# One core, two transformer-like blocks: ScalarE's order in the V projection, two DVE steps in stick-breaking attention, and one DMA for a broadcast

## The chip, the cores and the metric

The kernel runs on one core of a Trainium2 chip. The metric is the device time of one execution in microseconds (us); of several runs the median is given. The engines are TensorE (PE), VectorE (DVE), ScalarE (ACT), GpSimd (POOL) and SyncE (SP), which issues the weight loads. Each runs its own list of instructions in order and waits on semaphores for the others.

## The reference, cut to what matters

Two blocks follow each other, on 512 tokens of width 1024. The first has a mixer (a state-space part and a stick-breaking attention side by side), a cross attention to 256 memory tokens, and an MLP. The second, with 16 more tokens, has gated linear attention, sparse attention with a bias by distance, and two gated MLPs. What the change touches lies in the first block's mixer:

```python
def hybrid_mixer(hn, w_in, ...):
    proj = hn @ w_in
    z, xbc, dt_raw, qkv = jnp.split(proj, ...)
    xbc = silu(causal_dwconv(xbc, conv_w, conv_b))
    xs, bm, cm = jnp.split(xbc, ...)
    y = ssd_chunked(xh, dt, a, bm, cm)                 # 4 chunks of 128 tokens
    y = (y + d_skip * xh) * silu(z)
    y_ssd = rmsnorm(y, ssd_norm_g)
    q, k, v = jnp.split(qkv, 3, axis=-1)
    o = stick_breaking_attention(q, k, v)              # 8 heads of 64
    y_sb = rmsnorm(o, sb_norm_g)
    return concatenate([y_ssd, y_sb]) @ w_out

# stick-breaking, for s < t, with z = q k^T / 8:
# A[t,s] = sigmoid(z_ts) * prod_{s<j<t} (1 - sigmoid(z_tj));  out = A v

def memory_cross_attention(hn, mem, g_mem, w_q, w_k, w_v, w_o):
    m = rmsnorm(mem, g_mem)
    k, v = m @ w_k, m @ w_v
    ...

# second block, sparse attention: a bias by distance, one value per head and (key - query)
bias = rel_bias[rel_bucket(top_idx - qpos)]
```

## The kernel before, in words

All matrix products are float32 made of rounded parts: a value is split into a high part, `w_hi` or `x_hi`, and a low part, `w_lo` or `x_lo`, and PE adds hi x hi, hi x lo and lo x hi. Weights come in units of 128 x 2048 values. SP loads a unit into one of two places in `w_raw`, ACT makes `w_hi` (line 363), DVE `w_lo` (line 370), and PE multiplies (line 448). A layer has some units, a unit some tiles; tile (j, m) is tile m of unit j. A tile is summed in one of two PSUM slots, `lin[0]` or `lin[1]`, by turns, so PE starts a tile only when the tile before the last has been taken out (semaphores `lin_taken0` and `lin_taken1`).

The first block projects xbc, dt, z, q, k and v in that order, in float32 on 512 tokens. V is laid out with tokens in partitions: 2 units of 4 tiles, each 128 x 256, 24 matmuls a tile. ACT takes a tile into `v_tok` (line 905). Between the tiles other work is woven in, written by hand as tables `after={(unit, tile): step}`: for PE a step follows the tile, for ACT it goes ahead of the taking of the tile. In V these are, on ACT, the exponentials of the state-space part's last chunk (`act_ssd(act, 3)`: `seg`, `to_end`, `e_cum`), the Silu of z (`z_silu`, with its table load), the square roots of the memory norm (`act_memory_root`, with a table load), two constants copied to `sb_fixed`, the high parts of attention heads 0 and 1 (`act_sb_hi`: `sb_q`, `sb_k`), and the first logarithm (`act_sb_log`: `stay_e`). On PE they are the state-space step of chunk 3 with the sums of the memory norm after tile (0,2), and the logits of head 0 (`pe_sb_first`) after tile (1,0). DVE has a plain list in `dve_projections`: products of `q_t` and `k_t` with the norm's scale, low parts (`dve_sb_lo`), the state-space output (`dve_ssd_out`), the reciprocal of the memory norm (`dve_root`) and the products of `y_t` with the Silu.

The attention itself is `pe_stick`, `act_stick`, `dve_stick` and `pool_stick`, eight heads one behind the other. For each head PE makes logits (lines 1227 to 1231), ACT absolute value, exponential and logarithm (`stay_e`), DVE `stay`, ACT and DVE its two parts (`stay_hi`, `stay_lo`), PE the exponents (line 1247), ACT the weights `w_att`, and PE the product with `v_tok` (line 1257). PE fills its waits with other products in one PSUM bank, the fill bank: in heads 0 to 3 the memory's keys and values, in heads 4 to 7 the eight tiles of the state-space half of the output projection (`mixed`, line 1302). DVE empties the bank into `tmp` (line 1444), and PE may begin the next fill only then. After each pair of heads the output goes to `o_t`, ACT makes its `x_hi` (line 597) and DVE its `x_lo` (line 614).

POOL, in `pool_stick`, writes a vector of 655 distances for each of 8 heads, which lies in `tmp`, to DRAM, in 128 copies each (`rel_dram`): one small DMA from `tmp` to row 0 and, when that has landed, one DMA from row 0 to rows 1 to 127. DVE waits for them (`rel_kept`) before it overwrites `tmp` in head 4.

Of the kernel before, what the change touches and what calls it, by code (L numbers as in the profile page):

```python
# [23 lines left out]
P = 128  # L24
# [105 lines left out]
def build(nc, weights, x_t, mem_t, meta_t, cols, consts, w_a2b, rel_t, rel_dram, out):  # L130
# [4 lines left out]
    with ctx:  # L135
# [726 lines left out]
        def act_projections(act):  # L862
            def all_squares():
                for t in range(KD):
                    act_squares(act, l_mix, t, t % 2)

            act_evacuate(act, XBC, lambda j, i, m, s: nc.scalar.activation(
                conv_in[:, 4 * i + 2 * j + m, 3:3 + S1], psum_tile(s, S1), ACT.Copy),
                after={(0, 0): all_squares, (1, 1): lambda: act_root(act, l_mix)})
            next_hi(act, DT, 0, 0)  # L870

            def softplus():

                slot, before, _ = DT.tile(0, 0, 0)
                act.wait_ge(sem(f"lin_taken{slot}"), before + 1)
                bias = param("dt_bias", 0, 8)
                link(act, nc.scalar.activation(dt_row[:, 0, :], dt_row[:, 1, :], ACT.Abs, bias=bias))
                nc.scalar.activation(dt_row[:, 2, :], dt_row[:, 1, :], ACT.Relu, bias=bias)
                nc.scalar.preload_act_table_set("natural_log_exp_and_others")
                nc.scalar.activation(decay_rate[:, :], param("a_log", 0, 8), ACT.Exp)  # L880
                link(act, nc.scalar.activation(dt_row[:, 0, :], dt_row[:, 0, :], ACT.Exp, scale=-1.0))
                nc.scalar.activation(dt_row[:, 1, :], dt_row[:, 0, :], ACT.Ln, bias=1.0)\
                    .then_inc(sem("dt_log"), 1)

            def conv_silus():
                for t in range(6):
                    act.wait_ge(sem("conv_sum"), t + 1)
                    nc.scalar.activation(conv_out[:, t, :], conv_out[:, t, :], ACT.Silu)\
                        .then_inc(sem("conv_done"), 1)

            def z_silu():
                act.wait_ge(sem("z_scaled"), 1)
                nc.scalar.activation(zs[:, :, :], zs[:, :, :], ACT.Silu).then_inc(sem("z_silu"), 1)

            act_evacuate(act, Z, lambda j, i, m, s: nc.scalar.activation(
                zs[:, 2 * j + m, :], psum_tile(s, S1), ACT.Copy),
                after={(0, 0): softplus, (1, 0): conv_silus, (1, 1): lambda: act_ssd(act, 0)})
            act_evacuate(act, Q, lambda j, i, m, s: nc.scalar.activation(
                q_t[:, 4 * i + 2 * j + m, :], psum_tile(s, S1), ACT.Copy, scale=SB_SCALE),
                after={(1, 0): lambda: act_ssd(act, 1)})  # L900
            act_evacuate(act, K, lambda j, i, m, s: nc.scalar.activation(
                k_t[:, 4 * i + 2 * j + m, :], psum_tile(s, S1), ACT.Copy),
                after={(0, 1): lambda: act_ssd(act, 2), (1, 0): lambda: act_memory_squares(act, 0),
                       (1, 1): lambda: act_memory_squares(act, 4)})
            act_evacuate(act, V, lambda j, i, m, s: nc.scalar.activation(
                v_tok[:, m, (2 * i + j) * 256:(2 * i + j) * 256 + 256], lin[s][:, 0, 0:256], ACT.Copy,
                scale=scale_tok[:, 0, m:m + 1]),
                after={(0, 0): lambda: act_ssd(act, 3), (0, 2): z_silu, (0, 3): lambda: act_sb_first(act),
                       (1, 0): lambda: act_memory_root(act), (1, 1): lambda: act_sb_second(act),
                       (1, 2): lambda: act_sb_log(act, 0)})  # L910

        def dve_projections(dve):
            def scaled(t):

                return nc.vector.tensor_tensor(t, t, scale_d[:, 0:S1], ALU.mult)
# [63 lines left out]
            wait_taken(dve, K)  # L979
            for t in range(4):  # L980
                scaled(q_t[:, t, :])
                scaled(k_t[:, t, :]).then_inc(sem("qk_scaled"), 1)
            dve_sb_lo(dve, 0)
            dve_ssd_out(dve, 3)
            next_lo(dve, V, 1, 0)
            dve_root(dve, l_mem)
            dve_sb_lo(dve, 1)
            dve.wait_ge(sem("z_silu"), 1)
            for t in range(4):
                nc.vector.tensor_tensor(y_t[:, t, :], y_t[:, t, :], zs[:, t, :], ALU.mult)\  # L990
# [2 lines left out]
        def pe_projections(pe):  # L993
# [9 lines left out]
                                                (1, 0): lambda: pe_ssd_back(pe, 2),  # L1003
                                                (1, 1): lambda: pe_ssd_front(pe, 3)})
            pe_linear(pe, V, x_hi, x_lo, after={(0, 2): lambda: pe_memory_sums(pe),
                                                (1, 0): lambda: pe_sb_first(pe)})


        memory_sums, memory_tok = lin[0][:, 1, 0:256], lin[0][:, 1, 256:258]
# [15 lines left out]

        def act_memory_root(act):
            act.wait_ge(sem("square_sums"), l_mem.idx + 1)
            act.wait_ge(sem("qk_scaled"), 4)
            nc.scalar.activation(scale_d[:, 0:MEM], memory_sums, ACT.Sqrt, bias=eps_col(EPS1), scale=1.0 / D)
            nc.scalar.activation(scale_tok[:, 1, 0:2], memory_tok, ACT.Sqrt, bias=eps_col(EPS1), scale=1.0 / D)\  # L1030
                .then_inc(sem("square_root"), 1)
# [138 lines left out]

        def act_sb_hi(act, hd):
            (own, other, s), t = sb_halves(hd), hd // 2
            act.wait_ge(sem("qk_scaled"), t + 1)
            if hd >= 2:
                act.wait_ge(sem("sb_logits"), hd - 1)
            nc.scalar.activation(sb_q[s][own, :], q_t[own, t, :], ACT.Copy)
            nc.scalar.activation(sb_k[s][own, 0, :], k_t[own, t, :], ACT.Copy).then_inc(sem("sb_hi"), 1)

        def act_sb_first(act):

            for x, name in enumerate(("ident", "drop_upto")):
                nc.scalar.activation(sb_fixed[:, x, :], const(name), ACT.Copy)
            act_sb_hi(act, 0)

        def act_sb_second(act):

            nc.scalar.preload_act_table_set("natural_log_exp_and_others")
            act_sb_hi(act, 1)

        def dve_sb_lo(dve, hd):  # L1190
            (own, other, s), t = sb_halves(hd), hd // 2
# [214 lines left out]
        def dve_stick(dve):  # L1406
# [44 lines left out]
            for hd in range(8):  # L1451
# [9 lines left out]
                    split_lo(dve, XK.unit0 + (hd if hd < 5 else 5) + 1, 0, nc.vector)  # L1461
                if hd >= 2 and hd % 2 == 0:
                    output(hd // 2 - 1)
                if hd < 2:
                    memory_keys(hd)
                if hd >= 4:
                    mixed(2 * hd - 7)
                if hd < 7:
                    stay_low(hd + 1)
                if hd in (4, 5, 6):  # L1470
                    dve_operand(dve, l_sb, hd - 4)
                if hd < 2:
                    for t in (2 * hd, 2 * hd + 1):
                        dve_operand(dve, l_ssd, t)
# [869 lines left out]
        def pool_stick(pool):  # L2344
# [4 lines left out]
            def add_square(N, t):  # L2349
# [2 lines left out]
                acc = squares[:, N.slots[0], 0:N.n]  # L2352
                nc.gpsimd.tensor_tensor(acc, acc, tmp[:, t % 2, 0:N.n], ALU.add).then_inc(sem("square_added"), 1)

            pool.wait_ge(sem("qk_scaled"), 4)
            pool.dma_start(rel_dram[:, 0:1, :], rel_vec.unsqueeze(1)).then_inc(sem("rel_row"), 16)
            pool.wait_ge(sem("square_added"), l_mem.added0 + l_mem.k)
            pool_sb_other(pool, 0)
            pool.wait_ge(sem("rel_row"), 16)
            pool.dma_start(rel_dram[:, 1:P, :], rel_dram[:, 0:1, :].broadcast_to([8, P - 1, VEC]))\  # L2360
                .then_inc(sem("rel_kept"), 16)
            pool_sb_other(pool, 1)
            clear(l_ssd, l_mix.idx + 1)
            pool.wait_ge(sem("square_added"), l_ssd.added0)
# [353 lines left out]
```

## Time and profile before

| | us |
|---|---|
| median of 3 runs | 2100.66 |
| lowest, highest | 2099.49, 2101.15 |
| the profiled execution | 2099.49 |
| its span (first to last instruction) | 2097.7 |
| PE busy in it | 2013.8 |
| DVE busy | 1051.5 |
| ACT busy | 745.5 |
| POOL busy | 248.5 |

The times in the rows are those of the profiled execution, from the start of its span. The mean granted clock of PE was 0.978 of full speed, 2.4 GHz. A matmul's busy time overlaps that of its neighbours; the step from one start to the next tells what it costs. "Idle before" in square brackets is the time that the engine stood still ahead of an instruction, with the instruction that ended it.

### The profile page before, as it was taken

Reading aid. Unit: us, or ns where it says so; the run is one execution under the profiler, and the core shown is the slowest. Engines: PE = TensorE matmul, PEld = TensorE weight load, DVE = VectorE, ACT = ScalarE, POOL = GpSimd, SP = SyncE. Lnnn points to the kernel's source line nnn. Section 1 sums busy time; section 2 is a strip of 40 time slices with the busy share of each in tenths; the row PEclk is TensorE's granted clock in tenths of the full one; section 3 lists DMA queues with packets and bytes.
Section 4 is the critical chain, followed back from the end, with each engine's and each line's share of the span. In section 5 each row is a group of like instructions: output and inputs, shape, how many; then the busy total and the mean of one; then the engine's idle time right before and its main releaser. Section 6 shows DMA issues by size and latency. Waiting matters only on the chain.

```text
span 2097.7 us, 28613 instructions
## 1 busy us (share of the span) xinstructions
PE 2013.8 (96%) x11546; PEld 1725.7 (82%) x11546; DVE 1051.5 (50%) x1348; ACT 745.5 (36%) x941; POOL 248.5 (12%) x208
## 2 busy tenths in 40 slices
PE   8999988999999999999999999999997899999996
PEld 6788765788888878998999999998884588888885
DVE  6668665544444544131543434345897553444434
ACT  4449734423132443223332222223535442222122
POOL 2012230200000210013100000001245010000001
PEclk9999999999999998998999999999998999999998
DMA  4223211222222221111222222222121022222221
GB/s 173 101 81 114 71 49 41 100 90 92 101 99 82 101 81 52 69 41 41 81 81 100 81 100 81 98 83 101 61 91 51 21 86 95 101 96 84 101 100 60
DMA packets 27823, 174.67 MB, mean 83 GB/s; under 512 B 4409, under 2 KB 4537, under 8 KB 7762
## 3 DMA queue, kind: packets, MB, share of 16 engines
q1 hardware_dynamic: 25680, 167.32, 22.5%
q0 software_dynamic: 1888, 5.90, 0.9%
q8 instruction: 71, 1.16, 0.2%
q14 instruction: 22, 0.18, 0.0%
q10 hardware_dynamic: 162, 0.10, 0.0%
HBM read 171.19 MB, written 4.78 MB: 84 GB/s over the span
## 4 chain that ended last, share of the span: by engine, by line
PE 70%; issue 20%; DVE 5%; ACT 3%; POOL 2%; DMA 1%; SPq 0%; POOLq 0%; DVEq 0%; ACTq 0%
PE lin L448 57%; PE aux L1302 1%; PE aux L2176 1%; POOL squares L629 1%; ACT w_hi L363 1%; PE aux L1745 1%; PE aux L1759 1%; PE lin L1257 1%; PE lin L2146 1%; PE aux L2160 1%; DMA w_raw<-in_weights 1%; PE aux L1286 1%; DVE w_lo L370 1%; PE aux L1773 0%; PE aux L2024 0%
## 5 line engine op out<-in xcount | busy, mean ns | idle before, releaser
L448 PE MATMUL lin<-v_hi,w_hi 128*128 128x264 f32 (+1 forms) x1712 | 573.9, 335 | 4.8 <-DVE v_lo L614 3.5
L448 PE MATMUL lin<-v_hi,w_lo 128*128 128x264 f32 (+1 forms) x1712 | 571.1, 334 | 0.0
L448 PE MATMUL lin<-v_lo,w_hi 128*128 128x264 f32 (+1 forms) x1712 | 569.5, 333 | 0.0
L448 PE MATMUL lin<-x_hi,w_hi 128*128 128x512 f32 (+1 forms) x1176 | 417.0, 355 | 15.8 <-DVE tmp L542 6.6
L370 DVE TENSOR_TENSOR w_lo<-w_raw,w_hi 128x2048 fp32r<-128x2048 f32 (+1 forms) x144 | 328.5, 2281 | 187.0 <-ACT w_hi L363 186.8
L448 PE MATMUL lin<-x_hi,w_lo 128*128 128x512 f32 (+1 forms) x1176 | 413.7, 352 | 0.0
L448 PE MATMUL lin<-x_lo,w_hi 128*128 128x512 f32 (+1 forms) x1176 | 413.4, 352 | 0.0
L363 ACT ACTIVATE w_hi<-w_raw 128x2048 fp32r<-128x2048 f32 (+1 forms) x155 | 292.9, 1890 | 281.4 <-PE lin L448 274.3
L448 PEld LDWEIGHTS lin<-v_hi,w_hi 128*128 128x128 f32 x1712 | 324.6, 190 | 40.4 <-DVE v_lo L614 4.3
L448 PEld LDWEIGHTS lin<-v_lo,w_hi 128*128 128x128 f32 x1712 | 324.3, 189 | 33.6 <-issue 0.7
L448 PEld LDWEIGHTS lin<-v_hi,w_lo 128*128 128x128 f32 x1712 | 324.3, 189 | 32.1
L448 PEld LDWEIGHTS lin<-x_hi,w_hi 128*128 128x128 f32 x1176 | 222.8, 189 | 53.3 <-issue 7.7
L629 POOL TENSOR_TENSOR squares<-squares,tmp 128x512 f32<-128x512 f32 (+2 forms) x72 | 96.6, 1341 | 1321.1 <-ACT tmp L609 1318.5
L448 PEld LDWEIGHTS lin<-x_lo,w_hi 128*128 128x128 f32 x1176 | 223.2, 190 | 31.2 <-issue 0.5
L448 PEld LDWEIGHTS lin<-x_hi,w_lo 128*128 128x128 f32 x1176 | 223.2, 190 | 30.7
L1938 DVE TENSOR_TENSOR tmp<-tmp,lin 128x528 f32<-128x528 f32 (+1 forms) x44 | 30.7, 697 | 212.1 <-PE lin L448 212.1
L1917 ACT ACTIVATE x_hi<-tmp 128x528 f32 (+3 forms) x44 | 28.1, 640 | 218.6 <-DVE tmp L1938 218.6
L542 DVE TENSOR_TENSOR tmp<-lin,scale_d 128x512 f32<-128x512 f32 (+1 forms) x56 | 39.0, 697 | 97.0 <-PE lin L448 97.0
L370 POOL TENSOR_TENSOR w_lo<-w_raw,w_hi 128x2048 fp32r<-128x2048 f32 x11 | 51.0, 4638 | 303.2 <-ACT w_hi L363 303.2
L1915 ACT ACTIVATE tmp<-tmp 128x528 f32<-128x528 f32 (+1 forms) x44 | 28.1, 639 | 143.7 <-DVE tmp L1934 143.7
L597 ACT ACTIVATE v_hi<-h,col 128x512 fp32r<-128x512 f32 (+1 forms) x40 | 29.2, 730 | 116.4 <-DVEq L529 71.7
L545 DVE TENSOR_TENSOR h<-h,tmp 128x512 f32 (+3 forms) x88 | 65.1, 740 | 10.9 <-DVE tmp L542 9.8
(375 smaller groups left out, 2351.7 us busy)
## 6 DMA issues: line engine op xcount, KB each, us to landing
w_raw<-in_weights SPq DMA_DIRECT2D x155, 1024.0 KB, 4.8
rel_by_distance<-rel_by_distance POOLq DMA_DIRECT2D x1, 2599.5 KB, 20.9
rel_bias<-rel_by_distance POOLq DMA_DIRECT2D x8, 264.0 KB, 3.0
h<-in_x_t SPq DMA_DIRECT2D x4, 512.0 KB, 8.1
out_t<-h SPq DMA_DIRECT2D x4, 512.0 KB, 2.8
o_t<-in_mem_t POOLq DMA_DIRECT2D x1, 1024.0 KB, 5.0
cst<-in_consts SPq DMA_DIRECT2D x1, 512.0 KB, 9.8
col<-in_cols ACTq DMA_DIRECT2D x1, 67.0 KB, 5.8
```

The costliest lines, as they stand in the source:

```text
L363: nc.scalar.activation(w_hi[:, s, 0:n], w_raw[:, s, 0:n], ACT.Copy).then_inc(sem("w_hi_ready"), 1)
L370: does.tensor_tensor(w_lo[:, s, 0:n], w_raw[:, s, 0:n], w_hi[:, s, 0:n].bitcast(F32), ALU.subtract).then_inc(sem("w_lo_ready"), 1)
L448: last = nc.tensor.matmul(o, a, b, start=(k % (L.kc // k_banks) == 0 and p == 0), stop=((k + 1) % (L.kc // k_banks) == 0 and p == 2))
L542: nc.vector.tensor_tensor(out_t, psum_tile(slot, L.n), like_psum(scale, L.n), ALU.mult)\
L545: nc.vector.tensor_tensor(ht, ht, out_t, ALU.add).then_inc(sem("h_added"), 1)
L597: nc.scalar.activation(N.hi(t), N.tile(t), ACT.Copy, scale=N.gain(t)).then_inc(sem("operand_hi"), 1)
L629: nc.gpsimd.tensor_tensor(acc, acc, tmp[:, s, 0:N.n], ALU.add).then_inc(sem("square_added"), 1)
L1257: mm = nc.tensor.matmul(lin[1][64 * (hd % 2):64 * (hd % 2) + 64, 1, P * j:S1], v_tok[:, j, 64 * hd:64 * hd + 64], w_att[:, SB_AT[j]:SB_AT[ ...
L1286: mm = nc.tensor.matmul(o, memory_part(xp_, k)[:, m * P:m * P + P], wp[:, k, :], start=(k == 0 and q == 0), stop=(k == KD - 1 and q == 2))
L1915: nc.scalar.activation(g, g, ACT.Silu).then_inc(sem("gate_silu"), 1)
L1917: nc.scalar.activation(one(u_hi, t, 0, L.n), tmp[:, 2 + j, 0:L.n], ACT.Copy)\
L1938: nc.vector.tensor_tensor(like_psum(u, L.n), like_psum(g, L.n), psum_tile(up, L.n), ALU.mult)\
```

## The change

Five edits.

1. On ACT in V, the Silu of z moves from ahead of tile (0,2) to ahead of tile (0,0), right behind the last exponentials.
2. Also on ACT, the memory norm's roots move from ahead of (1,0) to ahead of (0,3), where they precede the `sb_fixed` copies; the load of the exponential's table follows at once, then head 0's high parts. Head 1's high parts move from (1,1) to (1,0). On PE the logits of head 0 move from behind tile (1,0) to behind tile (1,1).
3. On DVE, `dve_ssd_out(dve, 3)` comes ahead of head 0's low parts, and head 1's low parts ahead of the memory norm's reciprocal. `qk_scaled` is now raised once, behind all eight products, instead of four times.
4. In heads 4, 5 and 6 of the attention DVE makes `x_lo` of the attention's output ahead of `mixed(2 * hd - 7)` and `stay_low(hd + 1)`, instead of behind them.
5. POOL issues one DMA that writes all 128 copies from `tmp`, instead of two DMAs with a wait between them; a wait for the memory norm's squares goes too.

```diff
-            def z_silu():
+            def last_exp():
+                act_ssd(act, 3)
                 act.wait_ge(sem("z_scaled"), 1)
                 nc.scalar.activation(zs[:, :, :], zs[:, :, :], ACT.Silu).then_inc(sem("z_silu"), 1)
...
-                after={(0, 0): lambda: act_ssd(act, 3), (0, 2): z_silu, (0, 3): lambda: act_sb_first(act),
-                       (1, 0): lambda: act_memory_root(act), (1, 1): lambda: act_sb_second(act),
+                after={(0, 0): last_exp, (0, 3): lambda: act_sb_first(act), (1, 0): lambda: act_sb_hi(act, 1),
                        (1, 2): lambda: act_sb_log(act, 0)})
...
                 scaled(q_t[:, t, :])
-                scaled(k_t[:, t, :]).then_inc(sem("qk_scaled"), 1)
+                ins = scaled(k_t[:, t, :])
+            ins.then_inc(sem("qk_scaled"), 1)
+            dve_ssd_out(dve, 3)
             dve_sb_lo(dve, 0)
-            dve_ssd_out(dve, 3)
             next_lo(dve, V, 1, 0)
+            dve_sb_lo(dve, 1)
             dve_root(dve, l_mem)
-            dve_sb_lo(dve, 1)
...
             pe_linear(pe, V, x_hi, x_lo, after={(0, 2): lambda: pe_memory_sums(pe),
-                                                (1, 0): lambda: pe_sb_first(pe)})
+                                                (1, 1): lambda: pe_sb_first(pe)})
...
         def act_sb_first(act):
 
+            act_memory_root(act)
             for x, name in enumerate(("ident", "drop_upto")):
                 nc.scalar.activation(sb_fixed[:, x, :], const(name), ACT.Copy)
+            nc.scalar.preload_act_table_set("natural_log_exp_and_others")
             act_sb_hi(act, 0)
...
                     output(hd // 2 - 1)
+                if hd in (4, 5, 6):
+                    dve_operand(dve, l_sb, hd - 4)
                 if hd < 2:
                     memory_keys(hd)
                 if hd >= 4:
                     mixed(2 * hd - 7)
                 if hd < 7:
                     stay_low(hd + 1)
-                if hd in (4, 5, 6):
-                    dve_operand(dve, l_sb, hd - 4)
...
-            pool.wait_ge(sem("qk_scaled"), 4)
-            pool.dma_start(rel_dram[:, 0:1, :], rel_vec.unsqueeze(1)).then_inc(sem("rel_row"), 16)
-            pool.wait_ge(sem("square_added"), l_mem.added0 + l_mem.k)
+            pool.wait_ge(sem("qk_scaled"), 1)
+            pool.dma_start(rel_dram, rel_vec.unsqueeze(1).broadcast_to([8, P, VEC])).then_inc(sem("rel_kept"), 16)
             pool_sb_other(pool, 0)
-            pool.wait_ge(sem("rel_row"), 16)
-            pool.dma_start(rel_dram[:, 1:P, :], rel_dram[:, 0:1, :].broadcast_to([8, P - 1, VEC]))\
-                .then_inc(sem("rel_kept"), 16)
             pool_sb_other(pool, 1)
```

ACT's row in V before, from the last exponentials to the memory norm's root (`v_tok` is a tile taken, `zs` the Silu):

```order
L1100 ACTIVATE e_cum<-aux 128x512 x2
L905 ACTIVATE v_tok<-lin,scale_tok 128x256 x2
L893 ACT_TABLE_LOAD
L893 ACTIVATE zs<-zs 128x2048
L905 ACTIVATE v_tok<-lin,scale_tok 128x256
L1182 ACTIVATE sb_fixed<-cst 128x128 x2
L1176 ACTIVATE sb_q<-q_t 64x512
L1177 ACTIVATE sb_k<-k_t 64x512
L905 ACTIVATE v_tok<-lin,scale_tok 128x256
L363 ACTIVATE w_hi<-w_raw 128x2048
L1029 ACT_TABLE_LOAD
L1029 ACTIVATE scale_d<-lin,eps_t 128x256
```

The same place in the changed kernel:

```order
L1101 ACTIVATE e_cum<-aux 128x512 x2
L894 ACT_TABLE_LOAD
L894 ACTIVATE zs<-zs 128x2048
L906 ACTIVATE v_tok<-lin,scale_tok 128x256 x3
L1030 ACT_TABLE_LOAD
L1030 ACTIVATE scale_d<-lin,eps_t 128x256
L1031 ACTIVATE scale_tok<-lin,eps_t 128x2
L1183 ACTIVATE sb_fixed<-cst 128x128 x2
L1184 ACT_TABLE_LOAD
L1176 ACTIVATE sb_q<-q_t 64x512
L1177 ACTIVATE sb_k<-k_t 64x512
L906 ACTIVATE v_tok<-lin,scale_tok 128x256
```

The table load and the Silu now stand between the exponentials and the first tile taken, and two loads and the roots between the third and the fourth.

DVE's row in the attention before, from `stay` of head 7 (`tmp` is a fill taken, `x_lo` the low part of the attention's output):

```order
L1411 SCALAR_TENSOR_TENSOR stay<-lin,stay_e 128x1280
L370 TENSOR_TENSOR w_lo<-w_raw,w_hi 128x2048
L1421 COPY o_t<-lin 128x512
L1444 TENSOR_TENSOR tmp<-aux,rstd 128x512
L1416 TENSOR_TENSOR stay_lo<-stay,stay_hi 128x1280
L614 SCALAR_TENSOR_TENSOR x_lo<-o_t,col,x_hi 128x512
L1444 TENSOR_TENSOR tmp<-aux,rstd 128x512 x2
```

The same place in the changed kernel:

```order
L1408 SCALAR_TENSOR_TENSOR stay<-lin,stay_e 128x1280
L370 TENSOR_TENSOR w_lo<-w_raw,w_hi 128x2048
L1418 COPY o_t<-lin 128x512
L614 SCALAR_TENSOR_TENSOR x_lo<-o_t,col,x_hi 128x512
L1441 TENSOR_TENSOR tmp<-aux,rstd 128x512
L1413 TENSOR_TENSOR stay_lo<-stay,stay_hi 128x1280
L1441 TENSOR_TENSOR tmp<-aux,rstd 128x512 x2
```

The low part, which waits for ACT's `x_hi`, now stands ahead of the first `tmp`.

## Rows read from the trace of the kernel before

**Rows 1.** The page: busy time by engine, and the chain that ended last.

```profile
PE 2013.8 (96%) x11546; PEld 1725.7 (82%) x11546; DVE 1051.5 (50%) x1348; ACT 745.5 (36%) x941; POOL 248.5 (12%) x208
...
PE 70%; issue 20%; DVE 5%; ACT 3%; POOL 2%; DMA 1%; SPq 0%; POOLq 0%; DVEq 0%; ACTq 0%
```

**Rows 2.** Waits of PE, 140 to 280 us: total, times, longest.

```profile
PE aux L1247 <- DVE stay_lo L1416: 1.1, 1, 1.1
PE aux L1302 <- DVE tmp L1444: 1.0, 1, 1.0
PE aux L1227 <- ACT w_att L1354: 0.8, 1, 0.8
```

**Rows 3.** Timeline of PE in V: start, us, engine, line, what, count.

```profile
148.79 0.28 PE L448 MATMUL lin<-w_hi,x_hi 128*128 128x256 f32 x1
...
151.50 0.27 PE L448 MATMUL lin<-w_lo,x_hi 128*128 128x256 f32 x1
152.34 1.09 PE L1079 MATMUL aux<-seg,xdt 128*64 128x128 f32 x16 [0.56 <-DVE xds L1127]
...
172.11 0.39 PE L1227 MATMUL lin<-sb_q,sb_k 128*128 128x256 f32 x1 [0.56 <-ACT v_tok L905]
```

**Rows 4.** Timeline of ACT in V and behind it.

```profile
146.66 1.07 ACT L1100 ACTIVATE e_cum<-aux 128x512 f32<-128x512 f32 x2
147.62 0.47 ACT L905 ACTIVATE v_tok<-lin,scale_tok 128x256 f32<-128x256 f32 x1
148.99 0.48 ACT L905 ACTIVATE v_tok<-lin,scale_tok 128x256 f32<-128x256 f32 x1 [0.90 <-PE lin L448]
149.49 1.28 ACT L893 ACT_TABLE_LOAD   x1
150.78 1.91 ACT L893 ACTIVATE zs<-zs 128x2048 f32<-128x2048 f32 x1
...
171.59 0.47 ACT L905 ACTIVATE v_tok<-lin,scale_tok 128x256 f32<-128x256 f32 x1 [1.06 <-PE lin L448]
...
172.27 1.26 ACT L1338 ACTIVATE stay_hi<-stay 128x1280 fp32r<-128x1280 f32 x1
```

**Rows 5.** Timeline of DVE in V.

```profile
156.41 0.69 DVE L915 TENSOR_TENSOR k_t<-k_t,scale_d 128x512 f32<-128x512 f32 x1
...
170.20 1.49 DVE L1411 SCALAR_TENSOR_TENSOR stay<-aux,stay_e 128x1280 f32<-128x1280 f32 x1
```

**Rows 6.** Timelines of ACT, DVE and PE in the attention, heads 4 and 6.

```profile
236.23 0.71 ACT L597 ACTIVATE x_hi<-o_t,col 128x512 fp32r<-128x512 f32 x1
...
261.33 0.70 ACT L597 ACTIVATE x_hi<-o_t,col 128x512 fp32r<-128x512 f32 x1
...
238.83 1.78 DVE L614 SCALAR_TENSOR_TENSOR x_lo<-o_t,col,x_hi 128x512 fp32r<-128x512 f32 x1
...
261.95 0.69 DVE L1444 TENSOR_TENSOR tmp<-aux,rstd 128x512 f32<-128x512 f32 x1 [2.41 <-PE aux L1302]
...
277.75 0.75 DVE L614 SCALAR_TENSOR_TENSOR x_lo<-o_t,col,x_hi 128x512 fp32r<-128x512 f32 x1 [0.87 <-ACT x_hi L597]
...
238.21 0.45 PE L1302 MATMUL aux<-x_hi,w_hi 128*128 128x512 f32 x1
```

**Rows 7.** DMA issues, 130 to 290 us, KB and us to landing; DVE's timeline.

```profile
rel_by_distance<-rel_by_distance POOLq DMA_DIRECT2D x1, 2599.5 KB, 20.9
rel_by_distance<-tmp POOLq DMA_DIRECT2D x1, 20.5 KB, 1.9
...
228.78 0.69 DVE L1444 TENSOR_TENSOR tmp<-aux,rstd 128x512 f32<-128x512 f32 x1 [0.89 <-PE aux L1302]
```

**Rows 8.** Two stretches (length, busy, clock, DMA), and timeline of PE.

```profile
284.00:286.00 2.00, 0.00 (x0) 0.00 (x0) 1.97 (x2) 0.00 (x0) 0.00 (x0) 1.00 0.96 365
286.00:290.00 4.00, 3.60 (x9) 2.88 (x10) 3.07 (x5) 1.24 (x2) 1.39 (x1) 0.57 0.12 51
...
342.33 0.87 PE L1505 MATMUL aux<-cst,xp 128*128 128x128 f32 x6 [3.23 <-DVE xp L1559]
```

More of the change, by code:

```diff
@@ L1027, in act_memory_root @@
             act.wait_ge(sem("square_sums"), l_mem.idx + 1)
-            act.wait_ge(sem("qk_scaled"), 4)
+            act.wait_ge(sem("qk_scaled"), 1)
             nc.scalar.activation(scale_d[:, 0:MEM], memory_sums, ACT.Sqrt, bias=eps_col(EPS1), scale=1.0 / D)
@@ L1172, in act_sb_hi @@
             (own, other, s), t = sb_halves(hd), hd // 2
-            act.wait_ge(sem("qk_scaled"), t + 1)
             if hd >= 2:
@@ L1179, in act_sb_first @@
         def act_sb_first(act):
+            act_memory_root(act)
             for x, name in enumerate(("ident", "drop_upto")):
                 nc.scalar.activation(sb_fixed[:, x, :], const(name), ACT.Copy)
+            nc.scalar.preload_act_table_set("natural_log_exp_and_others")
             act_sb_hi(act, 0)
-        def act_sb_second(act):
-            nc.scalar.preload_act_table_set("natural_log_exp_and_others")
-            act_sb_hi(act, 1)
         def dve_sb_lo(dve, hd):
```

## The prediction

> **What bounds the kernel now.** I read the page first: a span of 2097.7 us of which TensorE (PE) is busy for 96%, and the chain that ended last lies on PE for 70% [rows 1]. So a change counts only where it makes PE start something later or earlier. The change lies between about 143 and 277 us, where the first block's V projection is followed by the stick-breaking attention. Then I read PE's waits in 140 to 280 us: 4.8 us in seven of them, none over 1.1 us; three of the seven are shown [rows 2]. There is hardly anything to win there, and anything that stops PE anew is lost time. Last I read the timelines of the engines beside each other. Through V's projection PE runs without a gap but for the 0.56 us before 152.34, in which it waits for `xds` [rows 3]. From 171.59 the end is set by ScalarE (ACT) instead: it takes V's last tile, and works without rest to `stay_hi` at 172.27 and on to `w_att`, for which PE waits at 184.57 [rows 2, 4]. That chain begins when PE finishes V, so V's delay passes through it whole. From there to 276 us PE is almost always the engine that is late.
>
> **Part 1, the Silu of z goes ahead of three evacuations.** V's tiles use two PSUM slots by turns, so PE may start tile (0,2) only when ACT has taken tile (0,0). Before, ACT ended the second exponential of `e_cum` at 146.66 + 1.07 = 147.73 and took that tile right behind it, until about 148.09; PE started tile (0,2) at 148.79 and lost nothing [rows 3, 4]. Now the table load and the Silu come between: 147.73 + 1.28 + 1.91 = 150.92, less 0.05 by which neighbouring activations overlap, then 0.47 for the evacuation: 151.34. PE follows an evacuation by about 0.05 us (it started at 172.11 after one that ended at 172.06 [rows 3, 4]), so at 151.39, which is 2.60 us later than before. Its work up to the state-space step then ends 2.60 us later as well, but there 0.56 us of waiting falls away, and some start-up between the pieces: from 151.50 (start of the tile's last matmul) plus 0.12 for one matmul, plus 2.60, it can start at 154.22, where it started at 152.34 [rows 3]. The net is **1.9 us**.
>
> Unknown here is whether the table load starts as soon as the exponentials end. In the row at 149.49 it begins 0.02 us behind the evacuation before it, and the Silu 0.01 us behind the load [rows 4]. The Trainium skill, "ScalarE: Activation LUTs", section "What ACT_TABLE_LOAD costs", adds about 1.38 us of draining to each switch. By that rule part 1 would cost about 3.3 us; the trace's load has no such gap on either side, so the row decides.
>
> **Part 2, the rest of V's order, at nothing, with its cover.** With PE 1.9 us late, tile (0,3) starts at 157.3 and unit 1 at 160.2. The memory norm's root now comes ahead of evacuation (0,3). It waits for the last scaled `k_t`, at 156.41 + 0.69 = 157.1 [rows 5], and then ACT does a load 1.28, the two roots 0.7, two copies for `sb_fixed` 0.5, a load 1.28 and the two casts of head 0, some 1.15: it ends at 162.0, and takes the tile by 162.4. (The load's row is shown [rows 4]; the small ones are ACT's rows of the same names at 152.96 to 165.61, ten of them.) Queued behind this on ACT is that tile, whose slot PE wants at 160.2 + 2.8 = 163.0: 0.6 us of cover. The next splits (1.9) and head 1's casts (1.1) end at 165.2, and tile (1,0) is taken by 165.6; PE wants that slot only after the first logits, which now stand behind tile (1,1), at 165.9 + 1.65 = 167.5. Head 0's low parts are asked for at 165.9 and are ready at about 163.5. On VectorE (DVE), split, head 1's parts, reciprocal and the four products with z follow each other to 172.1 and `stay` ends at 173.7, where it ended at 170.20 + 1.49 = 171.69 [rows 5]; ACT asks for it at 172.27 + 1.9 = 174.2 [rows 4]. That cover is 0.5 us. PE's work from 155.44 to 172.11 is the same in another order, and its number of table loads is three in both kernels. So part 2 adds 0. Without its covers it would add what is beyond them, at most about 1 us.
>
> **Part 3, `x_lo` ahead of `tmp`.** For heads 4, 5 and 6, DVE now makes the attention output's low part before it empties the fill bank into `tmp`. The low part waits for ACT's `x_hi`. In head 6 that ends at 261.33 + 0.70 = 262.03, DVE starts about 0.11 later, and the part itself takes 0.75 when nothing stands against it (0.68 to the next start) [rows 6]. So `tmp`, at 261.95 before, starts at 262.82 and ends at 263.51, and PE, which before waited 0.97 us for it, starts 0.86 later. In head 4: `x_hi` ends at 236.94, `tmp` at 238.41, PE 0.14 later at 238.55 instead of 238.21 [rows 6]: 0.34. Head 5 has the same rows 12.55 us on, 0.34 again. Sum: **1.5 us**. Behind `tmp` on DVE stand `stay_lo` and the next head's parts, which PE asks for over 3 us later.
>
> Its bounds: the one `x_lo` of 1.78 us at 238.83 ran beside GpSimd's (POOL's) addition [rows 6]. With that duration in all three places, 1.03 more each, part 3 costs 4.6 us. I take 0.75, since the new place lies ahead of POOL's addition. The lower bound is 0.86, if the two short ones vanish in start-up.
>
> **Part 4, one broadcast out of SBUF.** A copy of one row per head (landed in 1.9 us) and a DRAM broadcast (20.9 us) become one DMA of 1024 rows out of 8 partitions [rows 7]. POOL loses one issue, on which nobody waited. DVE needs the result where `tmp` is first overwritten, at 228.78, some 70 us after the issue at about 157.2 [rows 7]. No row shows 128 reads of one partition. Lower bound: the 20.9 us of the DRAM form, which costs nothing. Upper bound: the small copy's 1.9 us for each of its 128 repetitions, 243 us, which would hold DVE, and PE behind it, for some 170 us. I take nothing, by the row of equal size. The Trainium skill, "SBUF — State Buffer", section "Door 1: The DMA port swizzle", speaks against this edit: partitions 0 to 7 reach only two ports of about 27 GB/s each. As an estimate from that page the 2.6 MB would take about 49 us. No row of this trace shows it; the sum stays, the margin shrinks to about 20 us.
>
> **The sum.** 1.9 + 0 + 1.5 + 0 = 3.4 us. The profiled execution took 2099.49 us beside its span of 2097.7, so it would become 2102.9. That execution was the fastest of three whose median is 2100.66; compared median with median, the changed kernel comes to **2104.1 us**, 0.16% more. This kernel's measurement can tell about 0.2% (4.2 us) from no change, so the forecast lies close under that bound.
>
> **The rivals.**
> - *The clock falls behind the new stop.* PE now stands still for 2.6 us. Before, it stood for 2.76 us until 286.40, and the granted clock of 286 to 290 us was 0.57 of 2.4 GHz, with stretches at the lower level, 1.2 GHz [rows 8]; those 4 us gave 4 x 0.43 = 1.7 us less work. But ahead of 342.33 it stood for 3.23 us and the clock stayed at 1.00 [rows 8]. So about even odds, slightly less for a stop shorter than both. Sum 3.4 + 1.7 = 5.1: 2105.8.
> - *`x_lo` meets POOL* at 1.78 us in all three places: 1.9 + 4.6 = 6.5, 2107.2.
> - *The table load comes with a gap* that the row at 149.49 doesn't show. With 1.4 us in it (a mechanism that would apply at 147.73 because the exponentials, not an evacuation, stand ahead): 4.8, 2105.5.
> - *Only one part costs.* If the two 0.34 and the 0.86 are covered, 1.9: 2102.6; if ACT takes tile (0,0) in time, 1.5: 2102.2.
> - *The broadcast is late*: up to 170 us more, beyond 71 us of transfer.
> - *Not slower, by the clock.* PE has a dozen later stretches at 1.2 GHz; each like that at 286 us costs some 1.7 us. All work behind 277 us runs 3.4 us later than before, and if waits that just brought the clock down no longer do, each such stretch less returns 1.7. From two fewer on the changed kernel is not slower (3.4 against 3.4: 2100.7); five fewer would be needed for a measurable gain (8.5: 2095.6). For it: 2.76 us brought it down and 3.23 didn't, so it isn't length alone that decides. Against it: three runs agree within 1.66 us, so such stretches can't vary much.
>
> **How the numbers follow.** Forecast 0.40; clock behind the stop 0.28; `x_lo` beside POOL 0.09; table gap 0.03; one part only 0.09; late broadcast 0.03; not slower by the clock 0.08. The forecast alone reaches from 1.9 + 0.86 = 2.8 to about 4.4 with lost covers, 2103.4 to 2105.1, and the runs' own scatter is 0.8 to each side. The range 2101.6 to 2107.4 takes in the one-part cases and both slower ones, and leaves out the late broadcast and the favourable clock. Slower by over 0.2%, from 2104.9: a fifth of the forecast 0.08, most of the clock case 0.21, POOL 0.09, table 0.02, broadcast 0.03: 0.43. Faster: 0.05. Within: 0.52.
>
> **What would show it.** In the profile after, PE's timeline has a wait of 2.5 to 2.7 us on `v_tok` at about 151.4, and V's last tile is taken near 173.5 instead of 171.59. PE's waits show three on `tmp` in the fills, the longest about 1.8 us, two of 0.3. The rows of `rel_by_distance` show one DMA with a landing under 70 us. I am wrong in part 1 if PE starts tile (0,2) before 150 us, in part 2 if the distance from the 2.6 us wait to `stay_hi` grows, in part 3 if `tmp` still comes ahead of PE's need.

## The result: 0.4 to 0.6% slower, outside the range

| | median us | before on the same chip | ratio, 95% interval |
|---|---|---|---|
| the changed kernel | 2111.57 | 2099.49 | 1.0062 [1.0044, 1.0082] |
| the same, on a second chip | 2113.03 | 2103.55 | 1.0043 [1.0028, 1.0058] |

The forecast was 2104.1 us, in 2101.6 to 2107.4. The change costs some 9.5 to 12 us instead of 3.4. The rows below are of the profiled execution after: 2113.15 us, span 2111.3, mean clock 0.974.

The page's busy times and chain tell little [rows 1]: PE is busy for 8 us more, at a lower clock.

```profile
PE 2021.9 (96%) x11546; PEld 1730.5 (82%) x11546; DVE 1049.9 (50%) x1348; ACT 745.6 (35%) x941; POOL 247.9 (12%) x207
...
PE 70%; issue 20%; DVE 4%; ACT 3%; POOL 2%; DMA 1%; SPq 0%; POOLq 0%; DVEq 0%; ACTq 0%
```

PE's waits in 140 to 280 us (total, times, longest) tell more. Against [rows 2] three entries are new or longer: 2.4 us for `v_tok`, 2.0 for `tmp`, where 1.0 was, and 4.0 for `w_att`, where 0.8 was. In the last is a wait of 3.2 us, which no step of the prediction had.

```profile
PE aux L1224 <- ACT w_att L1351: 4.0, 2, 3.2
PE lin L448 <- ACT v_tok L906: 2.4, 1, 2.4
PE aux L1299 <- DVE tmp L1441: 2.0, 2, 1.8
PE aux L1244 <- DVE stay_lo L1413: 1.1, 1, 1.1
```

**V.** ACT's timeline [rows 4], then PE's [rows 3]:

```profile
146.49 1.06 ACT L1101 ACTIVATE e_cum<-aux 128x512 f32<-128x512 f32 x2
147.58 1.28 ACT L894 ACT_TABLE_LOAD   x1
148.87 1.91 ACT L894 ACTIVATE zs<-zs 128x2048 f32<-128x2048 f32 x1
150.69 0.82 ACT L906 ACTIVATE v_tok<-lin,scale_tok 128x256 f32<-128x256 f32 x2
...
174.97 0.47 ACT L906 ACTIVATE v_tok<-lin,scale_tok 128x256 f32<-128x256 f32 x1 [1.49 <-PE lin L448]
```

```profile
148.51 0.27 PE L448 MATMUL lin<-w_lo,x_hi 128*128 128x256 f32 x1
151.20 0.39 PE L448 MATMUL lin<-w_hi,x_hi 128*128 128x256 f32 x1 [2.41 <-ACT v_tok L906]
```

The stop is where it was forecast, and the table load follows the exponential after 0.03 us (146.49 + 1.06 = 147.55), so the rival of a gap there is out. Then the granted clock falls. In the windows (length, busy times, clock, DMA share, GB/s) of the changed kernel it is at 0.83 and 0.75, where it had been 1.00:

```profile
150.00:154.00 4.00, 2.80 (x18) 2.81 (x19) 3.97 (x8) 1.51 (x3) 0.00 (x0) 0.83 0.77 264
154.00:158.00 4.00, 4.00 (x45) 3.05 (x43) 2.93 (x5) 1.46 (x2) 0.77 (x1) 0.75 0.00 0
```

In the execution profiled on the second chip the stop is the same 2.41 us, and the clock stays:

```profile
150.00:154.00 4.00, 2.74 (x23) 2.74 (x24) 3.97 (x8) 1.57 (x3) 0.00 (x0) 1.00 0.68 264
154.00:158.00 4.00, 4.00 (x50) 3.09 (x50) 4.00 (x10) 1.40 (x2) 0.70 (x1) 1.00 0.00 0
```

**Head 2, the surprise.** The DMA rows after [rows 7] give the broadcast 56.7 us. It is issued at 157.23, so it runs until about 214:

```profile
w_raw<-in_weights SPq DMA_DIRECT2D x10, 1024.0 KB, 4.8
rel_by_distance<-tmp POOLq DMA_DIRECT2D x1, 2620.0 KB, 56.7
```

The median 4.8 us of the ten weight loads in 130 to 300 us hides the slow ones: three start beside the broadcast, at 167.15, 189.19 and 200.58, and land in 24.0, 24.1 and 15.4 us. The DMA view of 186 to 190 us alone shows the second, for unit 1 of the memory's values; it took 4.7 us before.

```profile
w_raw<-in_weights SPq DMA_DIRECT2D x1, 1024.0 KB, 24.1
```

SP's timeline has its issue:

```profile
189.19 28.95 SPq L2412 DMA_DIRECT2D w_raw<-in_weights  x3
```

189.19 + 24.1 = 213.3, and there ACT's and PE's timelines have this:

```profile
213.40 1.91 ACT L363 ACTIVATE w_hi<-w_raw 128x2048 fp32r<-128x2048 f32 x1 [5.98 <-PE aux L1283]
215.21 1.22 ACT L1351 ACTIVATE w_att<-aux 128x1280 f32<-128x1280 f32 x1
...
216.58 0.36 PE L1224 MATMUL aux<-sb_q,sb_k 128*128 128x256 f32 x1 [3.21 <-ACT w_att L1351]
```

`w_hi` waits for its load, `w_att` of head 2 stands behind `w_hi` on ACT, and PE waits for `w_att`. The bracket at 213.40 names PE's products of line 1283, which ended at about 213.4 as well. But `w_hi` doesn't wait for them: in the kernel before it started at 203.93, ahead of the first of them at 204.05. Before, the same load had been issued at 185.80, had landed in 4.7 us, and lay ready for 13.4 us; an earlier one, issued at 163.34 beside the DRAM form of the broadcast, had taken 10.1:

```profile
163.34 22.79 SPq L2419 DMA_DIRECT2D w_raw<-in_weights  x2
w_raw<-in_weights SPq DMA_DIRECT2D x1, 1024.0 KB, 10.1
...
185.80 11.73 SPq L2419 DMA_DIRECT2D w_raw<-in_weights  x2
w_raw<-in_weights SPq DMA_DIRECT2D x1, 1024.0 KB, 4.7
...
203.93 1.90 ACT L363 ACTIVATE w_hi<-w_raw 128x2048 fp32r<-128x2048 f32 x1
```

In the second profile of the changed kernel, where the load was issued at 187.74 and took 24.0 us, and in experiment 2 below, the same row names the load:

```profile
211.82 1.91 ACT L363 ACTIVATE w_hi<-w_raw 128x2048 fp32r<-128x2048 f32 x1 [5.86 <-DMA w_raw<-in_weights]
```

**Heads 4 to 6** [rows 6]: PE behind `tmp` of head 4, then `x_hi` on ACT, `x_lo` and `tmp` on DVE and PE behind them in head 6.

```profile
246.37 0.47 PE L1299 MATMUL aux<-x_hi,w_hi 128*128 128x512 f32 x1 [0.17 <-DVE tmp L1441]
...
269.75 0.71 ACT L597 ACTIVATE x_hi<-o_t,col 128x512 fp32r<-128x512 f32 x1
...
270.58 0.75 DVE L614 SCALAR_TENSOR_TENSOR x_lo<-o_t,col,x_hi 128x512 fp32r<-128x512 f32 x1 [2.84 <-ACT x_hi L597]
271.25 0.68 DVE L1441 TENSOR_TENSOR tmp<-aux,rstd 128x512 f32<-128x512 f32 x1
...
272.08 0.47 PE L1299 MATMUL aux<-x_hi,w_hi 128*128 128x512 f32 x1 [1.83 <-DVE tmp L1441]
```

### The profile page after: what moved, and what is told of

It is laid out like the page before. It is cut to its first block, busy times and chain, and to the rows that moved or that the text cites. A ratio compares the mean times of both kernels' runs of the same rounds, so it can differ in the third digit from the quotient of the medians.

```text
span 2111.3 us, 28606 instructions
## 1 busy us (share of the span) xinstructions
PE 2021.9 (96%) x11546; PEld 1730.5 (82%) x11546; DVE 1049.9 (50%) x1348; ACT 745.6 (35%) x941; POOL 247.9 (12%) x207
## 4 chain that ended last, share of the span: by engine, by line
PE 70%; issue 20%; DVE 4%; ACT 3%; POOL 2%; DMA 1%; SPq 0%; POOLq 0%; DVEq 0%; ACTq 0%
PE lin L448 57%; PE aux L2173 1%; POOL squares L629 1%; PE lin L1254 1%; ACT w_hi L363 1%; PE aux L1299 1%; PE aux L1742 1%; PE aux L1756 1%; PE lin L2143 1%; PE aux L2157 1%; DMA w_raw<-in_weights 1%; PE lin L1244 1%; PE aux L1283 1%; PE aux L1770 0%; DVE w_lo L370 0%
## 5 line engine op out<-in xcount | busy, mean ns | idle before, releaser
L545 DVE TENSOR_TENSOR h<-h,tmp 128x512 f32 (+3 forms) x88 | 65.1, 740 | 10.4 <-DVE tmp L542 9.0
## 6 DMA issues: line engine op xcount, KB each, us to landing
rel_by_distance<-tmp POOLq DMA_DIRECT2D x1, 2620.0 KB, 56.7
```

The costliest lines, as they stand in the source:

```text
L545: nc.vector.tensor_tensor(ht, ht, out_t, ALU.add).then_inc(sem("h_added"), 1)
```

## How far each landmark moves

The clock makes whole times scatter, so I judge each kernel by landmarks in the ACT timeline of its one profiled execution: the start of the taking of V's last tile, and of `w_att` of heads 1, 2, 4 and 7. The first row is times in us, the others are shifts against it. The median stands beside the median of before on the same chip.

| kernel | V's last | head 1 | head 2 | head 4 | head 7 | median (before) | ratio, 95% interval |
|---|---|---|---|---|---|---|---|
| before | 171.59 | 194.60 | 205.74 | 233.93 | 271.07 | | |
| changed | +3.38 | +3.39 | +9.47 | +7.82 | +9.26 | 2111.57 (2099.49) | 1.0062 [1.0044, 1.0082] |
| changed, again | +1.93 | +1.94 | +7.90 | +6.31 | +7.84 | 2113.03 (2103.55) | 1.0043 [1.0028, 1.0058] |
| 1: changed, two DMAs | +3.57 | +3.58 | +3.56 | +3.59 | +6.64 | 2105.74 (2101.94) | 1.0018 [1.0006, 1.0030] |
| 2: one DMA alone | -0.09 | -0.07 | +5.55 | +5.09 | +5.07 | 2108.22 (2101.94) | 1.0027 [1.0014, 1.0040] |
| 3: V's order alone | +3.33 | +3.34 | +3.32 | +3.33 | +3.31 | 2105.91 (2101.94) | 1.0015 [1.0001, 1.0029] |
| 4: x_lo first alone | -0.01 | 0.00 | -0.02 | -0.01 | +3.04 | 2104.07 (2101.94) | 1.0008 [0.9995, 1.0021] |
| 5: half the copies | -0.05 | -0.04 | -0.04 | -0.03 | -0.03 | 2100.49 (2101.87) | 0.9987 [0.9973, 1.0000] |
| 6: 128 partitions | -0.06 | -0.06 | -0.07 | -0.06 | -0.08 | 2100.37 (2101.87) | 0.9986 [0.9974, 0.9997] |
| 7: changed, 128 partitions | +3.57 | +3.58 | +3.57 | +3.58 | +6.66 | 2106.41 (2103.55) | 1.0009 [0.9995, 1.0023] |
| 8: V's order, Silu back | +1.19 | +1.59 | +1.58 | +1.60 | +1.60 | 2104.61 (2101.87) | 1.0010 [0.9994, 1.0026] |
| 9: values first | -0.01 | -0.01 | -0.02 | -0.01 | -1.21 | 2100.42 (2101.87) | 0.9996 [0.9980, 1.0011] |
| 10: before, again | -0.18 | -0.17 | -0.19 | -0.17 | -0.17 | 2106.20, one run | |
| 11: 6 and 9 together | +0.05 | +0.07 | +0.05 | +0.06 | -1.14 | 2100.63 (2103.55) | 0.9979 [0.9968, 0.9991] |

## The experiments

**1. The changed kernel with the two DMAs of before.**

```diff
-            pool.dma_start(rel_dram, rel_vec.unsqueeze(1).broadcast_to([8, P, VEC])).then_inc(sem("rel_kept"), 16)
+            pool.dma_start(rel_dram[:, 0:1, :], rel_vec.unsqueeze(1)).then_inc(sem("rel_row"), 16)
...
+            pool.dma_start(rel_dram[:, 1:P, :], rel_dram[:, 0:1, :].broadcast_to([8, P - 1, VEC]))\
+                .then_inc(sem("rel_kept"), 16)
```

> The changed kernel with the two DMAs of before (the small copy from tmp, then the broadcast inside DRAM) in place of the one broadcast out of SBUF. Theory A (the one DMA takes 57 us, slows the weight loads beside it and so w_hi of the cross attention's unit 1): the load at 188 us lands in about 5 us, w_att of head 2 comes 3.4 us later than before instead of 9.5, and V's stop, the clock behind it and x_lo alone are left: 3.4 + 1.45 = 4.9 us up to the end of the attention, 2103.0 to 2106.5. Theory B (the order in V and the attention, or the clock, cost the 12 us, and the broadcast is beside them): it stays at 2110 to 2113 and head 2 still comes 9 us late.

The load issued at 189.37 landed in 4.9 us and head 2 came 3.56 us late, no longer 9.47. Theory A holds. The clock fell twice in this execution, behind V's stop and behind the wait for `tmp` in head 6, so the landmark at head 7 is 6.64 us late and not the 4.9 expected.

**2. Before, with the one broadcast alone.**

```diff
-            pool.dma_start(rel_dram[:, 0:1, :], rel_vec.unsqueeze(1)).then_inc(sem("rel_row"), 16)
+            pool.dma_start(rel_dram, rel_vec.unsqueeze(1).broadcast_to([8, P, VEC])).then_inc(sem("rel_kept"), 16)
```

> The kernel before with only the one broadcast out of SBUF. Theory A: the DMA lands in about 57 us, a weight load issued beside it lands in about 24 us instead of 5, PE waits anew in head 2, about +4 us there and some more behind it where the clock falls, 2103.5 to 2109. Theory B: within 1 us of before, since the load has slack when nothing ahead of it has moved.

Theory A again. The broadcast landed in 57.3 us, the load in 23.7, and here the row names the load as the releaser:

```profile
209.48 1.91 ACT L363 ACTIVATE w_hi<-w_raw 128x2048 fp32r<-128x2048 f32 x1 [5.53 <-DMA w_raw<-in_weights]
```

**3. Before, with V's order alone** (edits 1 to 3 whole, of which a line each).

```diff
-                after={(0, 0): lambda: act_ssd(act, 3), (0, 2): z_silu, (0, 3): lambda: act_sb_first(act),
+                after={(0, 0): last_exp, (0, 3): lambda: act_sb_first(act), (1, 0): lambda: act_sb_hi(act, 1),
...
-                                                (1, 0): lambda: pe_sb_first(pe)})
+                                                (1, 1): lambda: pe_sb_first(pe)})
```

> The kernel before with only the new order in V (Silu first, roots and tables, DVE's order, the logits of head 0 one tile later). Theory A: PE stops for 2.4 us before tile (0,2), net 1.9, and the clock falls behind it, so V's last tile is taken 3.4 us later and the time is 3.4 us over before, 2102 to 2104.5. Rival: the stop is taken back later, since waits behind it go, within 1 us of before.

The landmarks give 3.3 us, none of it taken back up to head 7. The median is 4.0 us over before, with an interval of 0.2 to 6.1 us, so it agrees but tells little by itself.

**4. Before, with `x_lo` first alone** (edit 4).

```diff
+                if hd in (4, 5, 6):
+                    dve_operand(dve, l_sb, hd - 4)
                 if hd < 2:
                     memory_keys(hd)
```

> The kernel before with only x_lo ahead of tmp in heads 4 to 6. Theory A: three waits of PE on tmp of about 0.4, 0.4 and 1.8 us, 1.45 us in all, none elsewhere: 2100.5 to 2102. Rival: the longest wait brings the clock down, +3 us. Other rival: nothing, since PE's waits of before take it up.

PE's waits on `tmp` are close to those forecast (0.17 us in head 4 and 1.83 in head 6; the list shows no third), but in this execution the clock fell behind the wait of 1.83 us (0.58 in 264 to 268 us), as in experiments 1 and 7, so head 7 came 3.04 us late, not 1.45. In both executions of the changed kernel it did not fall there. So the first rival, the clock, holds in three of the five profiled executions that have this wait.

**5. Half the copies out of SBUF.**

```diff
+            pool.dma_start(rel_dram[:, 0:64, :], rel_vec.unsqueeze(1).broadcast_to([8, 64, VEC])).then_inc(sem("rel_kept"), 16)
...
+                shifted = bass.AP(tensor=rel_dram.tensor, offset=hd * P * VEC + P - 1, ap=[[0, 2], [VEC - 1, 64], [1, T2]])
```

> The kernel before with the one broadcast out of SBUF in half size, 64 copies; the sparse attention reads these 64 rows twice, in place of rows 64 to 127, so its bias is another. Overlap theory (only a load that runs beside the broadcast is slow, and only the one at 188 us lacks slack): it lands in about 28.5 us, at about 187 us, the load issued at 188 us lands in 5 us, w_att of head 2 comes at 205.7 as before, time within 2 us of before. Rival (the load is slow or the time lost for another reason, as the missing wait between the two DMAs): head 2 still comes 5 us late.

The sparse attention then reads 64 rows twice, so the bias it computes is not that of the reference. Nothing up to head 7 uses it.

The DMA rows of its trace, of 130 to 290 us and of 186 to 190 us:

```profile
rel_by_distance<-tmp POOLq DMA_DIRECT2D x1, 1310.0 KB, 29.1
...
w_raw<-in_weights SPq DMA_DIRECT2D x1, 1024.0 KB, 4.7
```

Half the bytes take half the time, the load behind them is quick, and every landmark is where it was. This kernel too has one DMA and no wait between two, so the rival falls. A load issued at 163.25, beside the broadcast, landed in 23.3 us here and moved no landmark. So a load beside the broadcast is slow, and it costs time only where it has less slack than that, as the one at 186 us in experiment 2.

**6. All copies out of SBUF, from 128 partitions.**

```diff
             pool.wait_ge(sem("rel_row"), 16)
-            pool.dma_start(rel_dram[:, 1:P, :], rel_dram[:, 0:1, :].broadcast_to([8, P - 1, VEC]))\
-                .then_inc(sem("rel_kept"), 16)
+            pool.dma_start(rel_wide, rel_dram[:, 0:1, :].broadcast_to([8, 16, VEC])).then_inc(sem("rel_row"), 16)
+            pool.wait_ge(sem("rel_row"), 32)
+            pool.dma_start(rel_dram.rearrange("h (r c) v -> (h r) c v", c=8),
+                           rel_wide.unsqueeze(1).broadcast_to([P, 8, VEC])).then_inc(sem("rel_kept"), 16)
```

> The kernel before with the 128 copies made out of SBUF, but from 128 partitions: row 0 goes to DRAM as before, then 16 copies of each head's row into 128 partitions of tmp, then 8 copies out of each partition. Port theory (eight partitions give some 46 GB/s to DMA, and that holds 57 us): the big transfer lands in 12 to 20 us, the weight load at 188 us in about 5 us, w_att of head 2 comes as before, time within 2 us of before. Packet theory (a packet out of SBUF takes four times one within DRAM, whatever its partition; they were 0.80 us against 0.21 us): it stays at 50 us or more, and the load is late again, 2104 to 2109.

```profile
rel_by_distance<-tmp POOLq DMA_DIRECT2D x1, 2620.0 KB, 11.8
tmp<-rel_by_distance POOLq DMA_DIRECT2D x1, 327.5 KB, 4.7
rel_by_distance<-tmp POOLq DMA_DIRECT2D x1, 20.5 KB, 1.9
```

The same 2620 KB (of 1024 bytes) leave SBUF in 11.8 us: 227 GB/s, against 47 in the 57.3 us from eight partitions. Packets out of SBUF are not slow as such, so the packet theory falls. That the limit is a port, and not something else that eight partitions share, was only argued: a source of eight partitions spread over others wasn't tried.

The run also changed two things at once: how many partitions are read, and how much of the DMA engines' time is used. In the windows below (length, busy times, clock, DMA share, GB/s) the three forms move with no weight load beside them: experiment 2 (eight partitions, half of the engines' time, 50 GB/s), the kernel before (within DRAM, half, 198 GB/s) and this kernel (all of it, 388 GB/s).

```profile
193.00:198.00 5.00, 5.00 (x43) 4.93 (x42) 4.27 (x4) 5.00 (x6) 0.00 (x0) 1.00 0.48 50
173.00:178.00 5.00, 3.93 (x29) 3.67 (x28) 4.44 (x9) 5.00 (x12) 0.11 (x1) 1.00 0.51 198
169.00:173.00 4.00, 3.44 (x28) 3.19 (x27) 2.35 (x3) 2.93 (x5) 0.00 (x0) 1.00 1.02 388
```

The DRAM form uses half of the engines' time too and is four times as fast, so the half isn't what makes the slow form slow. What is left of the difference is the source. The half does fit what happens to the load beside it. In experiment 2 the load is issued at 185.71. Its queue (hardware_dynamic) moves 0.52 MB, half of the load, in 186 to 191 us and nothing at all in 191 to 196, where only the broadcast's queue has packets (packets, MB, share of the engines' time):

```profile
q0 software_dynamic: 49, 0.26, 48.3%
q1 hardware_dynamic: 74, 0.52, 28.7%
...
q0 software_dynamic: 49, 0.26, 48.7%
```

So the load isn't slow evenly: one half goes through at once, the other is held back. That the held half is the one that falls to the engines which the broadcast keeps busy is inferred; the rows don't name the engine of a packet. The load issued at 163.3 us landed in 10.1 us beside the DRAM form (before) and in 23.9 beside the slow one (experiment 2). What the form out of 128 partitions costs a load beside it isn't measured: the load issued at 163.25 us landed in 5.2 us here, but the first packets of the transfer move only at about 167.3 us, when it was nearly done.

The median of this kernel is 1.5 us under before, though no landmark moved; that difference lies behind head 7 and has no cause on record.

**7. The changed kernel with this form.**

> The changed kernel with the copies made out of 128 partitions of tmp, in place of the one broadcast out of eight. Port theory: the load at 188 us lands in 5 us, w_att of head 2 comes at 209.1 instead of 215.2, and the time is that of the changed kernel with the two DMAs of before, 2104 to 2107. Rival (the new order needs the POOL queue free of the second and third DMA and of the waits between them, since POOL's additions for heads 0 and 1 stand behind them): stops of PE near 175 to 190 us, above 2108.

Landmarks as in experiment 1, load in 4.7 us. So the rest of the change does not need the one DMA: with three DMAs and their waits no new stop of PE appears.

**8. V's order with the Silu back ahead of tile (0,2).**

```diff
-                after={(0, 0): last_exp, (0, 3): lambda: act_sb_first(act), (1, 0): lambda: act_sb_hi(act, 1),
+                after={(0, 0): lambda: act_ssd(act, 3), (0, 2): z_silu, (0, 3): lambda: act_sb_first(act), (1, 0): lambda: act_sb_hi(act, 1),
```

> The new order in V, as in the experiment on it alone, but with the Silu ahead of tile (0,2) again. Theory (the whole of V's 3.4 us is the stop ahead of tile (0,2) and the clock behind it; the rest of the new order is covered): no wait of PE on v_tok near 151 us, V's last tile taken within 0.5 us of 171.6, time within 1.5 us of before. Rival (the other moves cost too): V's last tile 1 us or more late.

The rival holds. The stop at 151 us is gone, but PE waits at another place. ACT's roots ahead of tile (0,3) wait for `k_t` until 157.07, so this tile is taken only at 161.74, and PE needs its slot:

```profile
162.25 0.39 PE L448 MATMUL lin<-w_hi,x_hi 128*128 128x256 f32 x1 [1.02 <-ACT v_tok L905]
```

By V's end this costs 1.2 us, and 1.6 by head 1; at `stay_hi`, between the two, ACT waits 0.26 us for DVE's `stay`. In the changed kernel part 1's own delay of PE covers this: its list of waits has the one stop of 2.41 us on `v_tok` at line 448 and no second.

**9. Before, with the product of head 6 ahead of the fill in head 7.**

```diff
-                if hd >= 4:
+                if 4 <= hd < 7:
                     mixed(2 * hd - 8)
                 if hd:
                     values(hd - 1)
+                if hd == 7:
+                    mixed(2 * hd - 8)
```

> The kernel before with one change of its own: in head 7 PE makes the product with v_tok of head 6 ahead of the fill mixed(6) instead of behind it. In the kernel before PE waits 0.97 us for tmp at 262.8 us ahead of this fill while the weights of head 6, at 259.0, may be ready. If they are, the wait is filled and all behind it comes 0.5 to 1 us earlier, 0.5 to 1 us faster, which the landmarks show and the time hardly; if they are not, PE waits for w_att instead and nothing is won.

PE's wait on `tmp` is gone and head 7 comes 1.21 us earlier. The time alone can't show it.

**10. Before, profiled once more.**

> The kernel before, unchanged, profiled in another execution. Theory (the stretches at 1.2 GHz behind 285 us differ from one execution to the next of one and the same kernel): all landmarks up to 285 us within 0.2 us of the first profile, but the low stretches between 285 and 370 us or behind 1580 us may be others, 2098 to 2107. Rival (they belong to the change): the same 14 stretches at the same places, 2098 to 2101.

Up to head 7 all landmarks are the same within 0.2 us, and yet it took 2106.2 us against 2099.49. The window from 340 to 350 us, of the first profile and then of this one:

```profile
340.00:350.00 10.00, 6.53 (x33) 4.91 (x34) 5.32 (x9) 6.93 (x23) 0.00 (x0) 1.00 0.00 0
```

```profile
340.00:350.00 10.00, 7.28 (x20) 5.18 (x20) 4.11 (x8) 4.44 (x18) 0.00 (x0) 0.66 0.00 0
```

The same stretch of the program at clock 1.00 and 0.66, behind the same stop of PE of 3.23 us: the clock there isn't fixed by the kernel. So of the first pair's 13.7 us (2113.15 - 2099.49) the 9.3 up to head 7 are traced to the change. The 4.4 behind it are no more than what two executions of before differ by (6.7 us); that none of them comes from the change is not shown.

**The changed kernel again**, for the sum of the parts:

> The changed kernel, unchanged, beside the kernel before on the same chip, for the sum of the parts: V's order alone gave +4.0 us by the medians, x_lo ahead of tmp +2.1, the one broadcast +6.3, together 12.4. If they add, 2112 to 2115 where before is at 2101.9. In the profile the load at 188 us lands in 24 us again and w_att of head 2 comes at 215.2.

Load 24.0 us, `w_att` of head 2 at 213.64 instead of 215.2, since the clock stayed up in V. Its median lies 9.5 us over before, less than the 12.4 of the sum. The sum was of three medians, each uncertain by 2.5 us or more.

**11. Experiments 6 and 9 together, on before.**

> The kernel before with two changes of its own: the copies made out of 128 partitions, and the product with v_tok of head 6 ahead of the fill mixed(6) in head 7. Alone the first left everything up to 277 us as before (2100.4 against 2101.9 by the medians), and the second brought w_att of head 7 1.2 us earlier (2100.4 as well). Together: w_att of head 7 at 269.8 instead of 271.1, time 1 to 3 us under before. Rival: the scatter of the clock, some 4 us to each side, hides it.

2100.63 against 2103.55 us, ratio 0.9979 [0.9968, 0.9991]: some 0.1 to 0.3% under before by the medians. The landmarks account for 1.1 us of the 2.9; why the rest is there, or whether it is scatter, stays open.

## Why the prediction was wrong, step by step

- **Part 1** was right. Tile (0,2) was forecast 2.60 us late and PE's stop measured 2.41; net 1.9 forecast, 1.93 in the execution whose clock stayed up.
- **Part 2** at nothing was right for the whole change, for the reason given: 0.6 us of cover, which exists only because PE is 1.9 us late. Alone it costs 1.6 us (experiment 8), more than the "at most about 1 us" of the text.
- **Part 3** was right where the clock stayed up: 1.5 forecast, 9.26 - 7.82 = 1.44 and 7.84 - 6.31 = 1.53 measured. The rival beside it, `x_lo` at 1.78 us, did not come: all three took 0.75 us, where before all three had taken 1.78.
- **Part 4 is the step that failed.** Its cost was put at nothing, by the DRAM row of equal size, 20.9 us; the broadcast took 56.7, and it did cost 4.4 us net. The estimate of 49 us, worked out from the figure in the Trainium skill, "SBUF — State Buffer", section "Door 1: The DMA port swizzle", was much nearer, and I let the row decide although it showed another kind of source. But even with 57 us the text would have said nothing, because I held it against one deadline only, DVE's at 228.78, which it met. I did not ask what else moves on the DMA engines. A row of before could have warned me: the load issued at 163.34, beside the DRAM form, took 10.1 us. The load issued at 185.80 landed in 4.7 us, at 190.5, and `w_hi` used it at 203.93 without waiting: 13.4 us of slack. At 24.1 us it is 19.4 late, 6.0 more than the slack, and ACT stood still for 5.98. Of this 1.6 us comes back by head 4, in both executions of the changed kernel; the net is 7.82 - 3.39 = 4.4 in the first and 6.31 - 1.94 = 4.4 in the second. It includes low clock behind the stop (0.66 in 216 to 221 us of the first). Alone, on the kernel before, the broadcast costs 5.1 (experiment 2).
- **The clock rival** (chance 0.28) came true in four of the five profiled executions that have V's stop, the changed kernel's first and experiments 1, 3 and 7. In the two of the changed kernel V's end moved by 3.38 and by 1.93: 1.45 for the clock, where I had 1.7. My counterexample, the stop of 3.23 us ahead of 342.33 behind which the clock stayed at 1.00, did not hold for the next profile of the same kernel (experiment 10).
- **The sum** up to head 7, with what was measured for part 4: 1.9 + 0 + 4.4 + 1.5 = 7.8, and 9.3 with the clock behind V. Measured 7.84 and 9.26. Without the broadcast's 4.4 us the terms give 3.4, as forecast.
- **The scatter** was misjudged. I took 1.66 us from three runs. 29 runs of the kernel before on one chip went from 2097.4 to 2109.8 us. The argument that low stretches "can't vary much" fell with experiment 10.

## What to carry to other kernels

A long DMA has two prices: when it is done, and what it does to every transfer beside it; list the loads that it will overlap, with the slack of each. To copy a few rows many times, read from many partitions (11.8 us here) or within DRAM (20.9), not many times from a few (56.7). Where a profile's clock differs from that of its twin, compare landmarks ahead of the difference, and profile the old kernel twice before a story is built on one pair.

## What the hardware showed

- 2620 KB out of eight partitions: 56.7 to 57.3 us. Out of 128: 10.7 to 11.9. Within DRAM (2599.5 KB): 19.9 to 20.9.
- A 1 MB load issued while the slow one had 22 us or more to run: 23.3 to 24.1 us instead of 4.7 to 4.9. Beside the DRAM form: 9.0 to 10.4. None ran wholly beside the one out of 128 partitions. The load's data were on their way into SBUF and the broadcast's out of it; one half of the load went through at once and the other was held back (experiment 6).
- One stop of PE, 2.41 us at the same place, brought the clock down in four profiled executions and not in a fifth; one of 3.23 us did so in one execution of the kernel before and not in the other.
